# Delta rule of a transformer block: the triangular inverse on 32x32 blocks instead of 64x64

## The chip, the cores and the metric

One NeuronCore of one Trainium2 chip runs the whole program. The metric is device time in microseconds (us), the median of several runs. The kernel is written by hand, engine by engine, with semaphores: TensorE (PE in the profile), VectorE (DVE), ScalarE (ACT), GpSimd (POOL) and SyncE (SP), which issues the weight loads.

## The reference, cut to what matters

The reference is a stack of transformer layers on 256 context and 256 latent tokens, d_model 1024, with four feed-forward blocks. One of its mixers has an RWKV-7 half: 8 heads of 64 channels, each run once forward and once backward over the tokens.

```python
def step(S, inp):
    r, w, k, v, kk, a = inp
    S = (S * w[:, :, None, :]
         - jnp.einsum('bhvk,bhk->bhv', S, kk)[..., None] * (kk * a)[:, :, None, :]
         + v[..., None] * k[:, :, None, :])
    return S, jnp.einsum('bhvk,bhk->bhv', S, r)
```

The kernel does not step through tokens. It cuts them into 8 chunks of 64. Inside a chunk the rule becomes a linear system with a unit triangular 64x64 matrix I + A, where A holds products of decayed keys ("alpha", "beta"). The inverse of that matrix is applied to two right sides, and 8 chunk states are then chained.

## The kernel before, in words

The part that the change touches is called wkv in the code. Its work is 4 groups g (groups 0 and 1 forward, 2 and 3 backward). A group is two units u = 0, 1, and a unit is a pair of heads (128 partitions hold two heads, or two token halves). For each unit all 8 chunks of both heads are treated at once: 16 triangular matrices of 64x64, laid out as 8 cells of 64 columns on two partition halves (128x512). TensorE runs each group in three stages in a fixed order written by hand:

- **Start** (`wkv_start_tensor`). `within(n)` makes the 16 products beta x alpha and the 16 products alpha x beta (`products`, L2112, matmuls of 64x64x64). `turn` transposes the three factors (L2123), ScalarE copies them (L2281). Then come products with kappa and rho (`mixes`, L2112) and `key_values` (L2135). VectorE masks the results (L2423 to L2438), and starts the inverse: TI and its transpose TTI, both 128x512.
- **Levels** (`wkv_levels_tensor`). Five levels with block sizes 2, 4, 8, 16 and 32 double the block that is already inverted. Level li of unit u: GpSimd masks the strict triangle AT to the off-block of this level (MB, L2323, 128x512); TensorE multiplies MB by TI (`square`, L2177); ScalarE copies the product to XS (L2288); TensorE multiplies TTI by XS and XS by TTI; VectorE subtracts the two products from TI and TTI (L2445, L2446). The last level makes the second product alone. A `square` is 16 matmuls of 64x64x64, on the two diagonal 64x64 quadrants of the array. So a group has 28 squares.
- **Ends** (`wkv_ends_tensor`). TTI is applied to both right sides (L2208, L2213), ScalarE copies the solutions with a minus sign (L2302, L2303), and TensorE makes the outputs of the unit (L2224 to L2233) and the factors of the states (L2242 to L2251) from products on all four quadrants. VectorE adds the outputs (L2454, L2456) and the identity to the state factors (L2462). `within` of the next group waits for that.

After groups 1 and 3, `wkv_scan_tensor` (L2086, L2089) chains the 8 chunk states.

Beside that, the factors of the next group are prepared: two small products for decays and rates (`wkv_low_ranks`, L2100, L2101, in levels 0 and 2), sigmoids on ScalarE (`wkv_rates_scalar`), sums over the tokens on VectorE (`wkv_decay_sums`, L2413, L2415), exponentials on ScalarE (`wkv_decays_scalar`, L2272 to L2274), and products on GpSimd (`wkv_keys`, `wkv_factors`, `wkv_rho`, L2357 to L2378). The rates of the two units share one set of tiles, so unit 1 follows unit 0.

Every f32 matmul of this part stands in the trace as two MATMUL and two LDWEIGHTS records. "Records" below are MATMUL records. None of this part is in a hardware loop: every matmul is an instruction of its own in the program.

Of the kernel before, what the change touches and what calls it, by code (L numbers as in the profile page):

```python
# [27 lines left out]
P = 128  # L28
# [4 lines left out]
TT = T // P  # L33
# [10 lines left out]
CHUNK = 64  # L44
NCH = T // CHUNK
# [10 lines left out]
          ("sel_f", 64), ("mu", 7 * P), ("ml", 7 * P), ("cu", 6 * HD), ("cl", 6 * HD), ("su", HD), ("sl", HD), ("iu", HD),  # L56
          ("il", HD),
# [195 lines left out]
def build(nc, xin, ctx2, condrows, stream_k, stream_f, vecs, consts, tables, small, nabias, out):  # L253
# [4 lines left out]
    with ExitStack() as ctx:  # L258
# [1632 lines left out]
        NG1, NG2 = TI, MB  # L1891
# [9 lines left out]
        def rate_tiles(n):  # L1901

            return (SIG1, CUM1, AA1) if n == 1 else (SIG0, CUM0, AA0)
# [117 lines left out]
        LAST = len(BLOCK_LEVELS) - 1  # L2021

# [21 lines left out]

        def bank_pair(b, q):

            return banks[:, b:b + 2, q * 4 * HD:(q + 1) * 4 * HD].rearrange("p h (t c) -> p h t c", c=HD)

        def on_cells(mask):

            return mask.unsqueeze(1).unsqueeze(1).to_broadcast([P, 2, TT, HD])
# [52 lines left out]
        def wkv_start_tensor(pe, g):  # L2104
# [9 lines left out]

            def within(n):
# [34 lines left out]
            pe.wait_ge(factors_by_token, 3 * n0 + 1)  # L2150
            turn(n1, 1, 4)
            pe.wait_ge(factors_by_token, 3 * n0 + 2)
# [9 lines left out]
            pe.wait_ge(factors_by_token, 3 * n1 + 1)  # L2162
            mixes(n1, 6)
            pe.wait_ge(mixes_masked, n0 + 1)
            pe.wait_ge(factors_by_token, 3 * n1 + 2)
            key_values(n0, 4)
            pe.wait_ge(mixes_masked, n1 + 1)
            pe.wait_ge(factors_by_token, 3 * n1 + 3)
            key_values(n1, 5)

        def wkv_levels_tensor(pe, g):

            def square(bank, x, y):
                for i in range(2 * TT):
                    for half in HALF:
                        o = slice(i * HD, (i + 1) * HD)
                        mm = pe.matmul(pb[bank][half, o], x[half, o], y[half, o], start=True, stop=True)  # L2177
                return mm

            for li in range(len(BLOCK_LEVELS)):  # L2180
                for u in range(2):
                    q = NLEV * g + 2 * li + u
                    pe.wait_ge(level_masked, q + 1)
                    if li:
                        pe.wait_ge(t_updated, q - 1)
                    else:
                        pe.wait_ge(t_started, 2 * g + u + 1)
                    square(u, MB[u], TI[u]).then_inc(x_ready, 1)
                if g < 3 and li in (0, 2):
                    wkv_low_ranks(pe, 2 * g + 2 + li // 2)  # L2190
                for u in range(2):
                    pe.wait_ge(x_copied, NLEV * g + 2 * li + u + 1)
                    if li == 0:
                        pe.wait_ge(rho_masked, g + 1)
                        pe.wait_ge(kv_copied, 2 * g + u + 1)
                    if li < LAST:
                        square(2 + u, TTI[u], XS[u])
                    square(4 + u, XS[u], TTI[u]).then_inc(z_ready, 1)

        def wkv_ends_tensor(pe, g):  # L2200
            for u in range(2):
                pe.wait_ge(t_updated, NLEV * (g + 1) - 1 + u)
                if u and g < 3:
                    pe.wait_ge(rates_ready, 2 * g + 4)
                for tt in range(TT):
                    for hb in range(2):
                        for half in HALF:
                            pe.matmul(pb[2 + 4 * u][half, cell(hb, tt)], TTI[u][half, cell(hb, tt)],  # L2208
                                      TOKA[u][half, chunk(tt, hb)], start=True, stop=True)
                for tt in range(TT):  # L2210
                    for hb in range(2):
                        for half in HALF:
                            mm = pe.matmul(pb[3 + 4 * u][half, cell(hb, tt)], TTI[u][half, cell(hb, tt)],  # L2213
# [41 lines left out]
        def wkv_rates_scalar(act, n):  # L2255
# [5 lines left out]
            if n >= 2:  # L2261
                act.wait_ge(factors_ready, n)
# [13 lines left out]
        def wkv_scalar(act):  # L2276
            for g in range(4):
                for u in range(2):
                    for i, (by_token, bank) in enumerate(zip((TOKA, TOKB, TOKK), ((4, 5, 6), (7, 4, 5))[u])):
                        act.wait_ge(factors_turned, 3 * (2 * g + u) + i + 1)  # L2280
# [4 lines left out]
                for li in range(len(BLOCK_LEVELS)):  # L2285
                    for u in range(2):
                        act.wait_ge(x_ready, NLEV * g + 2 * li + u + 1)
                        act.activation(XS[u], pb[u][:, :], ACT.Copy).then_inc(x_copied, 1)  # L2288
                    if g == 3 and li < 4:
                        act.wait_ge(mixed_copied, pairs_before(1))  # L2290
                        act.activation(out_hi(0, li), H[:, li, :], ACT.Copy).then_inc(mixer_hi, 1)
                    if g < 3 and li == 0:
                        wkv_rates_scalar(act, 2 * g + 2)
                    if g < 3 and li == 2:
                        wkv_decays_scalar(act, 2 * g + 2)
                    if g < 3 and li == 4:
                        wkv_rates_scalar(act, 2 * g + 3)
# [6 lines left out]
                if g < 3:  # L2304
                    wkv_decays_scalar(act, 2 * g + 3)
# [8 lines left out]
        def wkv_gpsimd(pool):  # L2314

            def masks(g, li):
                level = C("cu" if g < 2 else "cl", LEVELS.index(BLOCK_LEVELS[li]) * HD, HD)
                for u in range(2):
                    if li:
                        pool.wait_ge(x_ready, NLEV * g + 2 * li + u - 1)  # L2320
                    else:
                        pool.wait_ge(triangles_ready, 2 * g + u + 1)
                    pool.tensor_tensor(cells(MB[u]), cells(AT[u]), on_cells(level), ALU.mult).then_inc(level_masked, 1)  # L2323
# [7 lines left out]
            for g in range(4):  # L2331
                n0 = 2 * g + 2
                masks(g, 0)
                masks(g, 1)
                if g < 3:
                    wkv_keys(pool, n0)
                masks(g, 2)
                masks(g, 3)
                if g < 3:
                    wkv_factors(pool, n0)  # L2340
                    if g != 1:
# [1277 lines left out]
```

## Time and profile before

| | |
|---|---|
| time, median of 3 runs | 2647.64 us (2647.13 to 2650.81) |
| span of the profiled execution | 2655.0 us |
| the four wkv groups, without the scan between groups 1 and 2 | 242.42 us |
| one group: start, levels, ends (group 0) | 12.26, 33.40, 15.54 us |
| TensorE busy | 2489.5 us, 94% |
| VectorE, ScalarE, GpSimd busy | 1696.8, 1059.9, 418.4 us |

For the profiled execution no time is given beside its span of 2655.0 us; the span is 7.4 us above the median of the other runs. TensorE's matmuls are pipelined and the ends of their records are modelled: a share of 94% says that it is seldom idle, not that it works at its peak. Where it is idle and the trace shows no one that it waits for, the profile writes "issue".

### The profile page before, as it was taken

To read this page: it belongs to the slowest core of one execution; us is meant where nothing else is said; L and a number is where in the kernel's file an instruction comes from. 1 tells how busy PE (TensorE), PEld (TensorE's weight loads), DVE (VectorE), ACT (ScalarE), POOL (GpSimd) and SP (SyncE) were. 2 spreads that over 40 slices of the span, in tenths; PEclk is the share of its full clock that TensorE was granted. 3 is DMA by queue.
4 is the path that set the end of the run, shared out by engine and by line. 5 is a ranking of instruction groups with operands and counts; after the bars stand their busy time and mean duration, and the time that the engine had idled before them with its cause. 6 is when DMAs were issued, how large, how long until landed. Compare 5 with 4: busy or idle time off the path is not lost.

```text
span 2655.0 us, 49488 instructions
## 1 busy us (share of the span) xinstructions
PE 2489.5 (94%) x19578; PEld 2041.4 (77%) x19578; DVE 1696.8 (64%) x2787; ACT 1059.9 (40%) x1750; POOL 418.4 (16%) x372
## 2 busy tenths in 40 slices
PE   6999999988888999999999999889999998899977
PEld 4888888757777778888788888669997875577857
DVE  2877787565554687778887754665555334565664
ACT  4222224454333542222522223455455343455344
POOL 2000001024445300000100001001013600121042
PEclk9999999989999999999999999999999999899999
DMA  7766662200000166666466652315563321023401
GB/s 264 226 194 193 195 204 94 81 5 4 4 4 12 56 195 192 193 194 201 157 205 193 194 149 89 98 51 159 181 180 104 96 91 40 1 64 123 126 14 48
DMA packets 88434, 323.55 MB, mean 122 GB/s; under 512 B 9712, under 2 KB 10864, under 8 KB 87504
## 3 DMA queue, kind: packets, MB, share of 16 engines
q1 hardware_dynamic: 86864, 310.68, 38.0%
q0 software_dynamic: 1408, 10.59, 1.1%
q8 instruction: 117, 1.92, 0.3%
q14 instruction: 45, 0.37, 0.0%
HBM read 320.18 MB, written 1.05 MB: 121 GB/s over the span
## 4 chain that ended last, share of the span: by engine, by line
PE 80%; DVE 9%; ACT 5%; issue 4%; DVEq 1%; DMA 1%; POOL 0%; POOLq 0%; ACTq 0%; SPq 0%
PE bank L502 21%; PE bank L504 21%; PE bank L503 21%; PE bank L2177 4%; PE bank L1389 1%; PE bank L1380 1%; DVE row_statistics L1434 1%; DVE weights_hi_lo L408 1%; PE bank L1405 1%; ACT work L1495 1%; ACT weights_hi_lo L403 1%; DMA weight_ring<-stream_k 1%; PE bank L1809 1%; ACT work L1504 1%; PE bank L2800 1%
## 5 line engine op out<-in xcount | busy, mean ns | idle before, releaser
L403 ACT ACTIVATE weights_hi_lo<-weight_ring 128x1024 fp32r<-128x1024 f32 (+1 forms) x381 | 396.7, 1042 | 1085.7 <-PE bank L504 1060.7
L408 DVE TENSOR_TENSOR weights_hi_lo<-weight_ring,weights_hi_lo 128x1024 fp32r<-128x1024 f32 (+1 forms) x374 | 454.6, 1216 | 481.4 <-ACT weights_hi_lo L403 479.7
L502 PE MATMUL bank<-input_hi,weights_hi_lo 128*128 128x512 f32 (+1 forms) x2032 | 743.8, 366 | 18.9 <-DVE input_lo L813 12.3
L503 PE MATMUL bank<-input_lo,weights_hi_lo 128*128 128x512 f32 (+1 forms) x2032 | 740.3, 364 | 0.0
L504 PE MATMUL bank<-input_hi,weights_hi_lo 128*128 128x512 f32 (+1 forms) x2032 | 740.1, 364 | 0.0
L502 PEld LDWEIGHTS bank<-input_hi,weights_hi_lo 128*128 128x128 f32 x2032 | 386.6, 190 | 85.7 <-issue 22.9
L503 PEld LDWEIGHTS bank<-input_lo,weights_hi_lo 128*128 128x128 f32 x2032 | 386.7, 190 | 60.2 <-issue 0.7
L504 PEld LDWEIGHTS bank<-input_hi,weights_hi_lo 128*128 128x128 f32 x2032 | 386.5, 190 | 59.9
L502 PE MATMUL bank<-hidden_hi_lo,weights_hi_lo 128*128 128x512 f32 (+1 forms) x952 | 343.5, 361 | 5.0 <-DVE hidden_hi_lo L1109 2.1
L504 PE MATMUL bank<-hidden_hi_lo,weights_hi_lo 128*128 128x512 f32 (+1 forms) x952 | 340.2, 357 | 0.0
L503 PE MATMUL bank<-hidden_hi_lo,weights_hi_lo 128*128 128x512 f32 (+1 forms) x952 | 340.2, 357 | 0.0
L754 POOL TENSOR_TENSOR work<-work 128x512 f32<-128x512 f32 (+1 forms) x48 | 70.6, 1470 | 1233.1 <-ACT work L642 1232.1
L552 DVE CUSTOM_DVE_ANT_0 work<-weight_ring,extra_tiles 128x1024 f32<-128x1024 f32 x176 | 224.6, 1276 | 35.8 <-issue 13.3
L553 DVE CUSTOM_DVE_ANT_0 weight_ring<-weight_ring,extra_tiles 128x1024 f32<-128x1024 f32 x176 | 214.9, 1221 | 0.0
L502 PEld LDWEIGHTS bank<-hidden_hi_lo,weights_hi_lo 128*128 128x128 f32 x952 | 181.2, 190 | 35.0 <-DVE hidden_hi_lo L1109 4.0
L503 PEld LDWEIGHTS bank<-hidden_hi_lo,weights_hi_lo 128*128 128x128 f32 x952 | 181.3, 190 | 26.0 <-issue 0.7
L504 PEld LDWEIGHTS bank<-hidden_hi_lo,weights_hi_lo 128*128 128x128 f32 x952 | 181.1, 190 | 25.6
L1279 DVE TENSOR_TENSOR work<-work,bank 128x512 f32<-128x512 f32 (+1 forms) x88 | 54.7, 622 | 54.4 <-PE bank L504 45.6
L1434 DVE TENSOR_REDUCE row_statistics<-bank 128x2 f32<-128x1024 f32 (+2 forms) x56 | 55.7, 995 | 38.8 <-PE bank L1380 36.8
L1495 ACT ACTIVATE work<-bank,row_statistics 128x512 f32<-128x512 f32 (+1 forms) x80 | 47.4, 598 | 68.3 <-DVE row_statistics L1434 47.2
L1389 PEld LDWEIGHTS bank<-constants,work 128*128 128x128 f32 x256 | 32.9, 160 | 51.0 <-issue 43.2
L2323 POOL TENSOR_TENSOR work<-work,constants 128x512 f32<-128x512 f32 x40 | 51.9, 1304 | 96.6 <-PE bank L2177 52.0
(515 smaller groups left out, 3110.9 us busy)
## 6 DMA issues: line engine op xcount, KB each, us to landing
weight_ring<-stream_k SPq DMA_DIRECT2D x498, 512.0 KB, 3.7
weight_ring<-stream_f SPq DMA_DIRECT2D x64, 448.0 KB, 3.4
weight_ring<-stream_f SPq DMA_DIRECT2D x32, 512.0 KB, 3.7
extra_tiles<-condrows POOLq DMA_DIRECT2D x3, 1024.0 KB, 9.3
constants<-consts POOLq DMA_DIRECT2D x1, 2112.5 KB, 9.0
residual_stream<-xin SPq DMA_DIRECT2D x1, 2048.0 KB, 12.1
work<-nabias POOLq DMA_DIRECT2D x1, 2048.0 KB, 8.9
residual_stream<-ctx POOLq DMA_DIRECT2D x1, 1024.0 KB, 6.2
```

What stands on the lines that cost most here:

```text
L403: act.activation(split_place(place)[:, 0, 0:words], w[:, 0:words], ACT.Copy).then_inc(hi_ready, 1)
L408: eng.tensor_tensor(split_place(place)[:, 1, 0:words], ring[:, n % RING, 0:words], split_place(place)[:, 0, 0:words].bitcast(F32), ALU.sub ...
L502: pe.matmul(out, weights[:, 0, w], x_hi, start=first, stop=False)
L503: pe.matmul(out, weights[:, 0, w], x_lo, start=False, stop=False)
L504: return pe.matmul(out, weights[:, 1, w], x_hi, start=False, stop=last)
L552: dve.tensor_tensor_reduce(PRODUCTS, w, COND[:, 0, :], 1.0, 0.0, ALU.mult, ALU.add, MOD_SUMS[:, j, 0:1])
L553: dve.tensor_tensor_reduce(w, w, COND[:, 1, :], 1.0, 0.0, ALU.mult, ALU.add, MOD_SUMS[:, j, 1:2]) .then_inc(mod_read, 1)
L754: pool.tensor_tensor(total, total, squares_of(place, kt)[:, a:b], ALU.add)
L1389: mm = pe.transpose(pb[4 + b][:, tok(i)], attention_probs(which, u)[:, b, tok(i)], C("ident"))
L1434: ins = dve.tensor_reduce(st[:, 0, :], sc[:, :, 0:nk], AX.X, ALU.max, negate=True)
L1495: ins = act.activation(attention_probs(which, it)[:, b, 0:nk], pb[2 * (it % 2) + b][:, 0:nk], ACT.Exp, bias=st[:, 0, b:b + 1], accum_out=s ...
L2177: mm = pe.matmul(pb[bank][half, o], x[half, o], y[half, o], start=True, stop=True)
```

## The change

- The recursion runs on 32x32 diagonal blocks alone. `within` becomes `near_products`: the two diagonal 32x32 blocks of each 64x64 matrix, in both orders, and a third set, the blocks beside the diagonal. These are matmuls with 64 rows, 32 weight columns and 32 moving columns.
- Levels 0 to 3 (block sizes 2 to 16) work on tiles of 128x256 (HALF_T = 256), four 32-row quarters with 8 blocks each. `square` becomes 32 matmuls of 32x32x32 on the four diagonal 32x32 tiles of the array.
- The last level computes only the block beside the diagonal: `across` and `across_turned` (16 matmuls each), and `near_blocks`, which moves the diagonal blocks to their place in a 128x512 bank by 32 matmuls with the identity and 16 with zeros. ScalarE copies that bank to INVERSE (in AT's tile), VectorE copies the off-blocks beside it.
- The copies XS go from ScalarE to VectorE, at 128x256; the updates of TI and TTI have a semaphore count each.
- GpSimd's masks (now 128x256) run up to two levels ahead, in two halves of MB, and all four levels of masks stand ahead of the rest of its work.
- Both units' rates are made together during the levels (in tiles of their own), then both `wkv_keys` on GpSimd. Both `wkv_decay_sums` stand behind the levels on VectorE, both `wkv_decays_scalar` behind the copies of the solutions on ScalarE, and `wkv_factors`, `wkv_rho` of both units follow on GpSimd.

```diff
+            def near_products(b, o, x, y, beside):
+                for tt in range(TT):
+                    for k in range(4):
+                        for hb in range(2):
+                            rows, i, j = HALF[hb], tt * P + k * SUB, tt * P + (k ^ beside) * SUB
+                            mm = pe.matmul(pb[b + hb][QUARTER[k], o + tt * SUB:o + (tt + 1) * SUB], x[rows, i:i + SUB],
+                                           y[rows, j:j + SUB], start=True, stop=True)
...
-                products(2 * (n % 2), 0, be, al)
-                products(2 * (n % 2), 1, al, be).then_inc(within_ready, 1)
+                near_products(2 * (n % 2), 0, be, al, 0)
+                near_products(2 * (n % 2), P, al, be, 0)
+                near_products(2 * (n % 2), 2 * P, be, al, 1).then_inc(within_ready, 1)
...
-            def square(bank, x, y):
+            def square(bank, x, x0, y):
                 for i in range(2 * TT):
-                    for half in HALF:
-                        o = slice(i * HD, (i + 1) * HD)
-                        mm = pe.matmul(pb[bank][half, o], x[half, o], y[half, o], start=True, stop=True)
+                    for rows in QUARTER:
+                        mm = pe.matmul(pb[bank][rows, near(i)], x[rows, x0 + i * SUB:x0 + (i + 1) * SUB], y[rows, near(i)],
+                                       start=True, stop=True)
+            def across(u):
+                for i in range(2 * TT):
+                    for k in first_rows(d):
+                        mm = pe.matmul(pb[u][QUARTER[k ^ 1], near(i)], AT[u][QUARTER[k], HALF_T + i * SUB:HALF_T + (i + 1) * SUB],
+                                       TI[u][QUARTER[k], near(i)], start=True, stop=True)
+            def near_blocks(u):
+                for i in range(2 * TT):
+                    for k, rows in enumerate(QUARTER):
+                        o = i * HD + k % 2 * SUB
+                        pe.matmul(pb[4 + u][rows, o:o + SUB], C("id32")[rows, :], TTI[u][rows, near(i)], start=True, stop=True)
+                for i in range(2 * TT):
+                    for k in first_rows(1 - d):
+                        o = i * HD + (1 - k % 2) * SUB
+                        mm = pe.matmul(pb[4 + u][QUARTER[k], o:o + SUB], C("id32")[QUARTER[k], :], C("zero32")[QUARTER[k], :],
+                                       start=True, stop=True)
...
 def wkv_scalar(act):
     for g in range(4):
...
-                for li in range(len(BLOCK_LEVELS)):
-                    for u in range(2):
-                        act.wait_ge(x_ready, NLEV * g + 2 * li + u + 1)
-                        act.activation(XS[u], pb[u][:, :], ACT.Copy).then_inc(x_copied, 1)
...
+                if g < 3:
+                    act.wait_ge(x_ready, NLEV * g + 2)
+                    wkv_rates_scalar(act, 2 * g + 2)
+                    wkv_rates_scalar(act, 2 * g + 3)
...
+                for u in range(2):
+                    act.wait_ge(z_ready, near_read(g, u))
+                    act.activation(INVERSE[u], pb[4 + u][:, :], ACT.Copy).then_inc(factors_by_token, 1)
...
+                    wkv_decays_scalar(act, 2 * g + 2)
                     wkv_decays_scalar(act, 2 * g + 3)
...
 def wkv_group_vector(dve, g):
...
-                    dve.wait_ge(z_ready, NLEV * g + 2 * li + u + 1)
                     if li < LAST:
-                        dve.tensor_tensor(TI[u], TI[u], pb[2 + u][:, :], ALU.subtract)
-                    dve.tensor_tensor(TTI[u], TTI[u], pb[4 + u][:, :], ALU.subtract).then_inc(t_updated, 1)
+                        dve.tensor_copy(XS[u][:, 0:HALF_T], pb[u][:, 0:HALF_T]).then_inc(x_copied, 1)
...
+                        dve.tensor_tensor(TI[u][:, 0:HALF_T], TI[u][:, 0:HALF_T], pb[2 + u][:, 0:HALF_T], ALU.subtract)\
+                           .then_inc(t_updated, 1)
```

## Rows read from the trace of the kernel before

**Rows 1.** The page, part 1: busy time, share of the span, records of TensorE.
```profile
PE 2489.5 (94%) x19578; PEld 2041.4 (77%) x19578; DVE 1696.8 (64%) x2787; ACT 1059.9 (40%) x1750; POOL 418.4 (16%) x372
```
**Rows 2.** Windows: busy (records) of PE, PEld, DVE, ACT, POOL. Group 0, group 3's levels.
```profile
605.88:618.14 12.26, 10.70 (x407) 9.67 (x409) 9.86 (x16) 3.75 (x7) 2.56 (x2) 1.00 0.02 4
618.14:651.54 33.40, 31.23 (x912) 28.18 (x908) 14.55 (x19) 13.12 (x19) 18.92 (x16) 1.00 0.02 4
651.54:667.08 15.54, 10.24 (x519) 9.72 (x514) 7.31 (x9) 7.70 (x13) 9.64 (x8) 1.00 0.02 4
...
814.60:844.50 29.90, 27.27 (x902) 26.75 (x900) 10.97 (x17) 9.59 (x16) 16.82 (x12) 1.00 0.02 4
```
**Rows 3.** The chain that ended last: us from the start, us, what. Levels of group 0.
```profile
642.33 4.89 PE bank L2177 x160
647.25 0.69 DVE spare_tiles L2445
...
648.68 3.02 PE bank L2177 x96
```
**Rows 4.** The same chain, in the ends of group 0.
```profile
657.70 0.47 PE bank L2224 x32
...
659.32 1.64 issue
660.96 0.46 PE bank L2242 x17
...
663.05 1.64 issue
```
**Rows 5.** Windows between these two stalls, TensorE alone.
```profile
657.23:659.35 2.12, 2.09 (x128) 1.00 0.04 8
660.95:663.08 2.13, 2.09 (x128) 1.00 0.03 8
```
**Rows 6.** DMA queue of the instructions: packets, MB; group 0, then one stall's period.
```profile
q8 instruction: 14, 0.23, 1.7%
q8 instruction: 1, 0.02, 2.2%
```
**Rows 7.** The chain, stalls in the ends of group 1.
```profile
720.95 1.36 issue
724.40 1.36 issue
```
**Rows 8.** Windows of whole groups, the first and the last of four, and their sum.
```profile
605.88:667.08 61.20, 52.17 (x1825) 47.58 (x1825) 31.72 (x44) 24.57 (x38) 31.11 (x26) 1.00 0.02 4
801.90:860.60 58.70, 53.18 (x1856) 48.73 (x1856) 25.97 (x42) 19.40 (x33) 33.28 (x23) 1.00 0.05 13
sum 242.42, PE 210.69 PEld 192.76 DVE 121.42 ACT 93.22 POOL 126.44; mean PE 52.67 PEld 48.19 DVE 30.36 ACT 23.30 POOL 31.61
```
**Rows 9.** Timeline, TensorE: 16 records in tiles of 128x32.
```profile
410.62 0.64 PE L488 MATMUL bank<-weight_ring,modulation 128*32 128x128 f32 x16
```
**Rows 10.** Source line L1467: VectorE's copy of 128x128 out of PSUM, ns min/median/max.
```profile
L1467 DVE COPY mixer_io<-bank x40: 277/285/292, 558.8 to 2571.0; 128x128 f32<-128x128 f32 x40
```
**Rows 11.** Windows with TensorE's granted clock (PEclk, 1.00 is full).
```profile
728.70:740.80 12.10, 7.57 (x208) 6.61 (x208) 8.39 (x20) 0.00 (x0) 0.00 (x0) 1.00 0.01 3
544.40:551.20 6.80, 4.97 (x16) 2.40 (x16) 3.54 (x8) 1.93 (x8) 0.00 (x0) 0.50 0.00 0
667.00:669.00 2.00, 1.92 (x65) 1.83 (x66) 0.00 (x0) 0.00 (x0) 0.00 (x0) 0.56 0.00 0
```
**Rows 12.** Timeline of group 0's ends: start, us, engine, what, idle before.
```profile
653.08 1.22 DVE L2413 TENSOR_TENSOR_SCAN work<-spare_tiles,work 128x512 f32<-128x512 f32 x1 [0.65 <-ACT work L2264]
654.37 1.54 DVE L2415 TENSOR_TENSOR work<-work 128x512 f32<-128x512 f32 x1
...
659.68 1.26 POOL L2368 TENSOR_TENSOR spare_tiles<-spare_tiles,projections 128x512 f32<-128x512 f32 x1 [1.72 <-ACT spare_tiles L2274]
665.69 1.29 DVE L2462 TENSOR_TENSOR projections<-bank,spare_tiles 128x512 f32<-128x512 f32 x2 [5.23 <-PE bank L2251]
```

More of the change, by code:

```diff
@@ L2021, in build @@
         LAST = len(BLOCK_LEVELS) - 1
+        NIN = 2 * LAST
+        NUPD = 4 * LAST + 4
+        NTOK = 8
+        QUARTER = [slice(SUB * k, SUB * k + SUB) for k in range(4)]
+        HALF_T = 2 * TT * SUB
         CORNERS = [(0, 0), (1, 1), (0, 1), (1, 0)]
@@ L2043, in by_half, with near, near_cells, near_bank_pair @@
             return ap.rearrange("p (t h c) -> p h t c", h=2, c=HD)
+        def near(i):
+            return slice(i * SUB, (i + 1) * SUB)
+        def near_cells(ap):
+            return ap[:, 0:HALF_T].rearrange("p (h t c) -> p h t c", h=2, c=SUB)
+        def near_bank_pair(b, o):
+            return banks[:, b:b + 2, o:o + TT * SUB].rearrange("p h (t c) -> p h t c", c=SUB)
+        def plain_update(g, li, u):
+            return NUPD * g + 4 * li + 2 * u + 1
+        def turned_update(g, li, u):
+            return NUPD * g + 4 * li + 2 * u + 2
+        def near_read(g, u):
+            return NUPD * g + 4 * LAST + u + 1
+        def across_read(g, u):
+            return NUPD * g + 4 * LAST + 2 + u + 1
+        def across_added(g, u):
+            return (NUPD - 2) * g + 4 * LAST + u + 1
+        def first_rows(d):
+            return (0, 2) if d == 0 else (1, 3)
         def bank_pair(b, q):
@@ L2178, in square, with across_turned @@
+            def across_turned(u):
+                for i in range(2 * TT):
+                    for k in first_rows(d):
+                        mm = pe.matmul(pb[u][QUARTER[k], near(i)], XS[u][QUARTER[k ^ 1], near(i)],
+                                       TTI[u][QUARTER[k ^ 1], near(i)], start=True, stop=True)
                 return mm
@@ L2195, in wkv_levels_tensor @@
                         pe.wait_ge(kv_copied, 2 * g + u + 1)
+                    elif li < LAST:
+                        pe.wait_ge(t_updated, turned_update(g, li - 1, u) - 2 * g)
                     if li < LAST:
-                        square(2 + u, TTI[u], XS[u])
-                    square(4 + u, XS[u], TTI[u]).then_inc(z_ready, 1)
+                        square(2 + u, TTI[u], 0, XS[u]).then_inc(z_ready, 1)
+                        square(4 + u, XS[u], 0, TTI[u]).then_inc(z_ready, 1)
+                    else:
+                        across_turned(u).then_inc(z_ready, 1)
         def wkv_ends_tensor(pe, g):
             for u in range(2):
-                pe.wait_ge(t_updated, NLEV * (g + 1) - 1 + u)
+                pe.wait_ge(t_updated, across_added(g, u))
+                pe.wait_ge(factors_by_token, NTOK * g + 6 + u + 1)
                 if u and g < 3:
```

139 lines of the change are left out of this document (82 added, 57 removed).

## Prediction, made before the changed kernel was run

> **What bounds the kernel now.** I read the page first: TensorE is busy 94% of the span [rows 1], so a stage is worth what it costs TensorE. Then the windows by stage. The four wkv groups take 242.42 us together [rows 8]; group 0 is 12.26 us of start, 33.40 of levels, 15.54 of ends [rows 2]. The reader should see that GpSimd, VectorE and ScalarE are busy for only 19, 15 and 13 of the 33.4 us of levels. The chain of waits there gives the pattern: TensorE runs 160 records in 4.89 us, VectorE's update of 0.69 and one more of some 0.6 follow, and the next stretch starts 6.35 us after the last (648.68 - 642.33) [rows 3]. A level has six squares of 32 records, 192 records; 4.89/160 = 30.6 ns a record with the run-out of the last one, about 29 without, 0.93 us a square; 6 of them leave some 0.7 us of a level in which TensorE waits or runs out. So the levels wait on TensorE, and the masks and copies are hidden. The two low-rank products cost 3.5 us: the levels of group 3, which has none, take 29.90 [rows 2].
>
> The decisive view is the chain in the ends. There the matmuls use four quadrants: 32 records in 0.47 us, 14.7 ns each. And twice TensorE stops for 1.64 us in the middle of a run of matmuls that waits for nobody, put down as "issue" [rows 4]. It starts again at 660.96 and at 664.69 (663.05 + 1.64), 3.73 us apart. Between two stops stand exactly 128 records [rows 5], and each has a weight load: 256 instructions. The queue that loads instructions brings one packet of 0.02 MB in such a period, and 14 in the group [rows 6], whose 1825 matmuls and 1825 weight loads [rows 8] make 14.3 times 256. I read this as follows: TensorE's program arrives in blocks of 256 instructions, and a new block takes about 3.6 us whatever the engine does meanwhile. The same stops in group 1: 720.95 + 1.36 and 724.40 + 1.36 are 3.45 us apart [rows 7]. The levels now use up a block in 128 x 29 ns = 3.7 us, just what the supply gives: they are at this limit already, without showing it.
>
> **The change, part by part.**
>
> *Levels on 32x32.* A square goes from 16 matmuls to 32, so from 32 records to 64. Each is shorter. No row shows a 32x32 tile; the nearest are these. A record with 64 moving columns holds its quadrant for 4 x 14.7 = 59 ns [rows 4]. 16 records in 32-column tiles with 128 moving columns take 0.64 us in all [rows 9], where one behind the other, at twice 59 ns, they would take 1.9: four tiles of this width run side by side. A record with 32 moving columns should hold its tile for half of 59 ns and a little more; I take 33, an estimate. Four quarters side by side make 8.2 ns a record, 0.52 us a square. Bounds: 14.7 ns (0.94 us a square, no gain) if a small record costs as much as one of 64 columns on four quadrants, and 33 ns (2.1 us) if the quarters do not overlap. I take 8.2 because [rows 9] shows such tiles overlap. The dependencies would allow a level of 6 x 0.52 plus 0.2 for the copy, 3.3 us instead of 6.35.
>
> *Last level.* across 32 records, near_blocks 96, across_turned 32, for two units 320, where 4 squares had 128. Levels in all: 24 squares x 64 + 320 = 1856 records instead of 28 x 32 = 896: +960. *within*: 3 x 64 instead of 2 x 32 for each unit: +256. Nothing else changes in number. So +1216 records per group on 1825, +4864 in all.
>
> *Copies on VectorE.* A 128x128 copy is 0.285 us [rows 10], an update of 128x512 0.69 [rows 3]; at 128x256 between, some 0.40. Six per level, 2.4 us: hidden behind even the short level of 3.3 us, and further behind a level that waits for instructions. In the longest case, 0.69 each, they are 4.1 us. Masks: GpSimd's share falls and runs ahead; now they are hidden too (18.9 of 33.4 us with all its other work [rows 2]). No gain or loss on TensorE's path.
>
> *Rates together, decays behind the levels.* After the levels VectorE makes two sums (1.22 + 1.54 each [rows 12]), 5.5 us, where it made one; ScalarE's exponentials of both units come after the copies of the solutions, the last of which ends some 5 us in (solves of 128 records at 29 ns, 3.7 us, then two copies), so at about 6.5 to 10 us into the ends; then GpSimd has two times factors (three products of 1.26 [rows 12]) and rho, until some 18 us. `within` of unit 0 needs its factors at 15.5 us, and they are there at 12; unit 1's are needed a `within` and three transposes later, 1.5 blocks or 5 us, at 21. So it is covered, by 3 us; without that cover (no instruction limit) it would be needed at about 19 and the margin would be 1 to 2 us. Queued behind the late sums on VectorE are the output adds; TensorE's wait on them ends only with L2462 at 665.69 [rows 12], 8 us later. Cost nothing; at worst 2 us a group.
>
> *The sum.* All four groups now have 1824 x 3 + 1856 = 7328 records; after it 12192, or 24384 instructions, 95.25 blocks. At 3.6 us a block (between the 3.45 of group 1 [rows 7] and the 3.73 of group 0 [rows 4]) that is 342.9 us. Minus 5 for the blocks that are at hand when group 0 and, after the scan, group 2 begin (two times 3.6 less 1.0 to run them); plus 2 for the wait on L2462 at the end of each group where it does not fall into a block's wait (0.5 each). 340 against 242.4 [rows 8]: +98. A block of the levels takes TensorE 1 us of work and at most 1.5 us of waits for copies, under 3.6, so that none of the dependencies adds.
>
> *Clock.* TensorE is at work for 1 us in 3.6 there. After the idle time before L2462 the clock was granted at 0.56 (1.2 GHz for most of the window), in sparse attention work at 0.50, but in the scan, where TensorE gets 208 short records in 12.1 us, it stayed at 1.00 [rows 11]. In the levels half a clock is hidden (2 us a block). It costs in the two-quadrant solves of the ends: a block of 128 records takes 7.4 us instead of 3.7. I count this in a third of cases: 4 x 3.7 / 3 = +5.
>
> So +103 us: the profiled execution 2655 + 103 = 2758; the median of the runs, 2647.6, lies 7.4 us below the profile's span, so 2751.
>
> *A, the supply of instructions is no limit* (the other side). The stops in the ends would come from something else, or blocks would arrive ahead. For it: in the levels there is hardly any stop now. Against: 128 records between stops, twice, and one instruction packet. Then levels 0 to 3 take 4 x 3.3, the two low-rank products 3.5, the last level 4.6 (320 records of 8 to 16 ns and a copy at each end, about its 4 squares of now): 21.3 instead of 33.4; within costs +1.3 (2 x (192 x 8.2 - 64 x 14.7) ns); -10.8 a group, -43: 2604 us. It decides once a block arrives in less than 61 us / 23.8 blocks = 2.5 us. The page "Runtime: NRT & Kernel Launch" of the Trainium skill, section "Instruction fetch mechanics", says the same: blocks of 256 instructions, fetched while the current one runs, the crossing "mostly hidden". The trace agrees on the block, and differs on the hiding [rows 4, 5]; the measurement decides.
>
> *B, a small record costs as much as a large one, and A.* 14.7 ns a record, levels 1856 x 14.7 = 27.3, with 3.5 and 2.5 of waits 33, as now; within +3.8 a group, +15: 2663 us. For it: no row below 14.7 ns holds for long.
>
> *C, the clock falls in every group*: solves +3.7, and the two low-rank blocks 3.5 more together with some 0.5 for key_values: 4 x 7.7 = +31 on the +98: 2776 us.
>
> *D, the quarters do not overlap*: 2240 records of levels and within at 33 ns are 73.9 us a group, by blocks 63.0: +11 a group, +44: 2789 us.
>
> **Numbers.** Forecast (blocks of 3.45 to 3.73 us, clock mostly full) 0.64; C 0.2; D 0.04; A 0.07; B 0.05. At 3.45 us a block the sum is 328.6 - 3 = 325.6, +83: 2731; at 3.73 355.3 - 3 = 352, +110, with C's 31 +141: 2789. The bounds of the unknown: packets that come somewhat faster when they are the only limit (3.3 us: 314 - 3, +69: 2716). Range 2712 to 2796. A measurement here tells 0.2%, 5 us, from no change. Slower: 0.64 + 0.2 + 0.04 + 0.05 = 0.93; faster 0.06, same 0.01 (A, with the late factors taking back all of its gain).
>
> **What would show it.** In the profile after: about 24400 / 256 = 95 instruction packets over the groups, a group of 83 to 90 us, levels of some 52 us and a start of some 18; stops put down as "issue" of 1.5 to 2.6 us every 128 records through the levels; squares of 0.5 us between them; VectorE, ScalarE and GpSimd waiting for TensorE. The prediction is wrong if levels run 192 times 2 records in clearly under 10 us, if packets come closer than 3.3 us, or if copies on VectorE end TensorE's waits.

## The result, and the profile after

The changed kernel takes 2774.12 us (median, 2772.39 to 2777.97), the kernel before 2648.62 (2647.13 to 2650.81) beside it: 1.0477 times as long (95% interval 1.046 to 1.0493). The prediction, 2751 us and a range of 2712 to 2796, was right in sign and range and 23 us short. One execution of the kernel with split columns below (2790.17 us) and one of the kernel before (3577.27 us) ran in a slower state, and every figure here leaves them out.

The page of the changed kernel: span and busy time of each engine (part 1), part 2's strip of 40 slices for TensorE and its granted clock, the instruction queue (part 3), and the shares of the chain (part 4).

```profile
span 2771.7 us, 59255 instructions
PE 2513.5 (91%) x24442; PEld 2057.9 (74%) x24442; DVE 1688.4 (61%) x2843; ACT 1036.6 (37%) x1712; POOL 387.5 (14%) x364
PE   6999999976676699999999999987999999889977
PEclk9999999996676599999999999999999999999999
q8 instruction: 155, 2.54, 0.4%
PE 78%; DVE 7%; issue 7%; ACT 4%; DMA 1%; DVEq 1%; POOL 0%; POOLq 0%; ACTq 0%; SPq 0%
```

Compare with [rows 1]: TensorE has 4864 more records and is busy for only 24 us more, while the span is 117 us longer. The digits show where: in the six slices that hold most of wkv TensorE is busy for 60 to 79%, and the granted clock falls with it. From 590 to 990 us the chain of waits holds 54 stops of more than 1.3 us put down as "issue", 99 us together, where that of before holds 6, 9 us together; these 90 us more are most of the 117. The packets of the instruction queue are the best check on what a packet is. The page of before counts 117. 38 more came, and 4864 records with as many weight loads, 9728 instructions, are 38.0 times 256.

Windows by stage: the four starts, the four levels, the four ends (first and last of each, and the sum of the four), and the whole group 0.

```profile
602.30:620.10 17.80, 13.83 (x664) 12.62 (x664) 8.84 (x18) 3.97 (x7) 3.02 (x4) 0.90 0.02 5
...
sum 78.52, PE 59.05 PEld 54.15 DVE 35.52 ACT 16.32 POOL 22.67; mean PE 14.76 PEld 13.54 DVE 8.88 ACT 4.08 POOL 5.67
620.10:676.10 56.00, 34.92 (x1869) 29.15 (x1864) 11.83 (x28) 5.61 (x8) 9.46 (x10) 0.58 0.02 4
...
909.28:960.73 51.45, 29.26 (x1860) 27.29 (x1856) 11.86 (x29) 4.82 (x8) 18.70 (x14) 0.56 0.02 5
sum 217.71, PE 132.44 PEld 113.35 DVE 47.37 ACT 21.65 POOL 47.06; mean PE 33.11 PEld 28.34 DVE 11.84 ACT 5.41 POOL 11.77
676.10:691.35 15.25, 11.79 (x513) 11.41 (x513) 8.44 (x12) 7.78 (x13) 5.25 (x6) 0.88 0.02 5
...
960.73:980.50 19.77, 16.53 (x520) 13.63 (x520) 5.01 (x9) 5.07 (x9) 4.86 (x3) 0.85 0.10 31
sum 68.77, PE 52.32 PEld 48.10 DVE 31.32 ACT 28.42 POOL 23.63; mean PE 13.08 PEld 12.03 DVE 7.83 ACT 7.10 POOL 5.91
602.30:691.35 89.05, 60.54 (x3041) 53.18 (x3041) 29.11 (x58) 17.36 (x28) 17.73 (x20) 0.69 0.02 4
```

Against [rows 2] a start grew from 12.26 to 17.80 us, levels from 33.40 to 56.00 (group 3: 29.90 to 51.45). Group 0's ends hardly changed (15.54 to 15.25), but in groups 1 to 3 they grew from 14.9 to 16.1 us before to 17 to 20. The four groups take 365.0 us (the three sums) instead of the 242.42 of [rows 8]: +122.6. The levels hold 87 us of it.

The chain of waits in the levels of group 0 (start us, us, what), where [rows 3] had stretches of 96 to 160 records and VectorE's updates between them:

```profile
628.33 2.09 issue
630.42 1.39 PE bank L2232 x106
631.80 2.68 issue
634.49 1.93 PE bank L2232 x127
636.41 1.79 issue
638.20 1.93 PE bank L2232 x95
640.13 2.34 issue
642.47 1.93 PE bank L2232 x127
644.40 2.06 issue
```

Windows of TensorE alone between these stops, the counterpart of [rows 5]:

```profile
634.49:638.20 3.71, 1.92 (x127) 0.50 0.02 4
638.20:642.47 4.27, 1.93 (x128) 0.50 0.02 4
642.47:646.46 3.99, 1.93 (x127) 0.50 0.02 4
```

This is the stop of [rows 4] again and again: 127 or 128 records, a stop that nobody ends, the next block 3.7 to 4.3 us after the last. L2232 is the 32x32 square. Who is waiting for whom around it, from the timeline (in brackets the idle time before, and who ended it):

```profile
634.49 0.79 PE L2232 MATMUL bank<-spare_tiles,work 32*32 32x32 f32 x41 [2.68 <-issue]
635.31 0.42 DVE L2536 COPY spare_tiles<-bank 128x256 f32<-128x256 f32 x1 [3.28 <-PE bank L2232]
635.36 0.73 POOL L2416 TENSOR_TENSOR work<-work,constants 128x256 f32<-128x256 f32 x1 [2.98 <-PE bank L2232]
636.17 0.42 DVE L2542 TENSOR_TENSOR work<-work,bank 128x256 f32<-128x256 f32 x1 [0.43 <-PE bank L2232]
```

VectorE had been idle for 3.28 us and GpSimd for 2.98, both waiting for TensorE; the copy XS on VectorE takes 0.42.

### The profile page after: what moved, and what is told of

Its sections match the earlier page's. It is cut to its first block, busy times and chain, and to the rows that moved or that the text cites. A ratio compares the mean times of both kernels' runs of the same rounds, so it can differ in the third digit from the quotient of the medians.

```text
span 2771.7 us, 59255 instructions
## 1 busy us (share of the span) xinstructions
PE 2513.5 (91%) x24442; PEld 2057.9 (74%) x24442; DVE 1688.4 (61%) x2843; ACT 1036.6 (37%) x1712; POOL 387.5 (14%) x364
## 3 DMA queue, kind: packets, MB, share of 16 engines
HBM read 320.01 MB, written 1.05 MB: 116 GB/s over the span
## 4 chain that ended last, share of the span: by engine, by line
PE 78%; DVE 7%; issue 7%; ACT 4%; DMA 1%; DVEq 1%; POOL 0%; POOLq 0%; ACTq 0%; SPq 0%
PE bank L503 20%; PE bank L504 20%; PE bank L505 20%; PE bank L2232 3%; PE bank L1390 1%; DVE weights_hi_lo L409 1%; DVE row_statistics L1435 1%; DMA weight_ring<-stream_k 1%; PE bank L1381 1%; ACT work L1496 1%; ACT weights_hi_lo L404 1%; PE bank L1406 1%; ACT work L1505 1%; PE bank L1810 1%; PE bank L2177 1%
## 5 line engine op out<-in xcount | busy, mean ns | idle before, releaser
L2232 PE MATMUL bank<-work 32*32 32x32 f32 x3072 | 48.3, 225 | 24.5 <-issue 24.5
L2232 PEld LDWEIGHTS bank<-work 32*32 32x32 f32 x3072 | 43.1, 138 | 33.6 <-issue 33.2
```

The lines of the kernel that those rows point to most:

```text
L2232: mm = pe.matmul(pb[bank][rows, near(i)], x[rows, x0 + i * SUB:x0 + (i + 1) * SUB], y[rows, near(i)], start=True, stop=True)
```

## The experiments

Two theories are weighed. One is the supply of instructions, as predicted. The other is that the records themselves hold TensorE, by what each costs. In the expectations F is the first theory and R the second. Each median is given with its range; every ratio is against the kernel before, measured beside it.

### Twice the instructions, the arithmetic unchanged

Before's `square`, with each 64-column matmul as two of 32 columns:

```diff
-                    for half in HALF:
-                        o = slice(i * HD, (i + 1) * HD)
-                        mm = pe.matmul(pb[bank][half, o], x[half, o], y[half, o], start=True, stop=True)
+                    for c in range(2):
+                        for half in HALF:
+                            o, m = slice(i * HD, (i + 1) * HD), slice(i * HD + 32 * c, i * HD + 32 * c + 32)
+                            mm = pe.matmul(pb[bank][half, m], x[half, o], y[half, m], start=True, stop=True)
```

> Kernel before, each square's matmul cut into two that move 32 of its 64 columns: same result, same columns, twice the instructions in the levels (+896 records, 7 blocks of 256 instructions a group). Theory F (the program arrives in blocks of 256 instructions, one per 3.5 to 3.8 us): a group has 2720 records, 21.25 blocks, 77 to 81 us instead of 61: +64 to +80 us, 2712 to 2729. Rival R (no limit on the supply; TensorE's columns and dependencies set the time): 32 columns hold a quadrant for 33 ns instead of half of 59, a square takes 1.06 us instead of 0.93: +15 us, 2663.

2743.05 us (2738.62 to 2746.11), 1.0347 (1.032 to 1.0374). The chain in the levels of group 0, and the window of its longest stretch:

```profile
616.52 1.05 PE bank L2100 x2
617.57 0.86 PE bank L2101 x2
618.43 22.52 PE bank L2178 x768
```
```profile
618.43:640.95 22.52, 22.52 (x770) 22.48 (x769) 7.47 (x10) 3.09 (x6) 7.41 (x6) 1.00 0.02 4
```

The time is far above R's 2663 us and 14 us above the top of F's range, and F's mechanism is not there: group 0's levels have no stop. 768 records in 22.52 us are 29.3 ns each, without one stop, at a granted clock of 1.00. That is the pace per record of [rows 3], where a record moves twice the columns. A record with 64 weight columns holds its quadrant for 59 ns whether it moves 32 or 64 columns. A block of 128 such records takes 3.75 us, within the supply's 3.3 to 4.3, so this run can't tell the two theories apart. It does show what R had wrong: halving the columns did not bring a record's 59 ns to 33.

### Half the columns, as many instructions

The square moves 32 of each 64 columns, and ScalarE and VectorE read each computed half twice. ScalarE's copy is scaled by 0, so in two squares of three one operand is all zeros:

```diff
-                        o = slice(i * HD, (i + 1) * HD)
-                        mm = pe.matmul(pb[bank][half, o], x[half, o], y[half, o], start=True, stop=True)
+                        o, m = slice(i * HD, (i + 1) * HD), slice(i * HD, i * HD + 32)
+                        mm = pe.matmul(pb[bank][half, m], x[half, o], y[half, m], start=True, stop=True)
...
-                        act.activation(XS[u], pb[u][:, :], ACT.Copy).then_inc(x_copied, 1)
+                        act.activation(halved(XS[u]), first_half(pb[u][:, :]), ACT.Copy, scale=0.0).then_inc(x_copied, 1)
```

> Kernel before, each square moves only 32 of its 64 columns; ScalarE's copy of the product is scaled by 0 and copies and updates read the written half twice, so the levels' result is left out and the inverse stays what it was at its start. Same instructions, half the columns. F: a level has 192 records, 1.5 blocks, so it can't fall below 5.4 us (6.35 before): -12 to -18 us, 2631 to 2637. R: squares of 0.53 us, the level then follows copies and updates, 4.7 us: -30 us or more, 2618 or less.

2713.58 us (2703.14 to 2719.24), 1.0246 (1.0226 to 1.0266): slower with half of the columns, which no theory had. A window of the second half of group 0's levels:

```profile
637.50:661.50 24.00, 24.00 (x451) 24.00 (x452) 5.83 (x9) 4.94 (x7) 7.71 (x8) 0.50 0.01 2
```

TensorE never stops in it, and its clock was granted at 0.50 (1.2 GHz). At 24.00/451 = 53 ns a record, two quadrants side by side, each is held for 106 ns, nearly twice the 59 of full clock. The levels of group 0 took 47.9 us. As a test of supply against records it is inconclusive; it shows what half a clock costs where nothing else limits.

Why the clock fell is open, and the narrower records alone don't explain it: the run before this one has records of the same shape, as tightly packed, at 1.00 for 22.52 us. Two things differ. Here one operand is zero in two squares of three; and before the clock fell, at about 624 us, TensorE had stood for 1.4 us (from 621.26) while VectorE made its two updates. Neither was tried alone; the written-out kernel below has such zeros too, and its clock from 620 to 676 us was 0.58, as without them. With these records it then stayed at 0.50 for the rest of the levels without a stop, and rose at about 665 us, in the solves, which move 64 columns.

### The new square with wider columns

The changed kernel, each 32x32 matmul moving 64 columns instead of 32:

```diff
+                        if i < 2 * TT - 1:
+                            m = slice(i * SUB, (i + 2) * SUB)
+                        else:
+                            m = slice((i - 1) * SUB, (i + 1) * SUB)
-                        mm = pe.matmul(pb[bank][rows, near(i)], x[rows, x0 + i * SUB:x0 + (i + 1) * SUB], y[rows, near(i)],
+                        mm = pe.matmul(pb[bank][rows, m], x[rows, x0 + i * SUB:x0 + (i + 1) * SUB], y[rows, m],
```

> Kernel after, each of its squares in levels 0 to 3 moves 64 columns instead of 32 (overlapping outputs, so the inverse is wrong): same instructions, twice the columns. F: a block of the levels needs about 2 us of TensorE at full clock, still under the 3.6 us in which the next arrives: no change, 2768 to 2782; if the additional activity keeps the clock up, up to 15 us faster. R: 1536 records a group cost 6.5 ns more at full and 13 at half clock, 10 to 20 us a group: +40 to +80 us, 2814 to 2854.

2772.31 us (2768.7 to 2773.76), 1.0458 (1.0439 to 1.0476), so no change against the changed kernel's 2774.12. The window of group 0's levels, and a stop and the block behind it from the chain:

```profile
619.75:675.75 56.00, 39.11 (x1868) 34.11 (x1865) 11.84 (x29) 5.61 (x8) 9.45 (x10) 0.82 0.02 4
```
```profile
642.00 1.98 PE bank L2236 x127
643.98 2.00 issue
```

56.00 us, as in the changed kernel, though the records do twice the columns and are busy for 39 us instead of 35. The clock was granted at 0.82 instead of 0.58, and that bought nothing. Neither the width of a record nor the clock sets the levels' time. R had 2814 us or more; here it is out.

### Fewer instructions: 48 matmuls of each unit moved to other engines

The changed kernel without `near_blocks` on TensorE: ScalarE copies the diagonal blocks to their place, GpSimd sets the zeros.

```diff
-                        near_blocks(u).then_inc(z_ready, 1)
...
-                    act.activation(INVERSE[u], pb[4 + u][:, :], ACT.Copy).then_inc(factors_by_token, 1)
+                    for k, rows in enumerate(QUARTER):
+                        ins = act.activation(block_of(u, k, k % 2), tiles(TTI[u][rows, 0:HALF_T], SUB), ACT.Copy)
...
+                    for k in first_rows(1 - g // 2):
+                        ins = pool.memset(block_of(u, k, 1 - k % 2), 0.0)
```

> Kernel after, without the 48 matmuls per unit that only move the diagonal blocks and zeros into place in the last level: ScalarE copies TTI's four quarters to their place instead, GpSimd writes the zeros. Same result. 192 records fewer a group, 1.5 blocks. F (supply of instructions): -1.5 x 3.7 us a group less a small wait for ScalarE's eight short copies, -14 to -22 us, 2752 to 2760. R (TensorE's own time): 192 records of 10 to 15 ns, and the new copies stand on the path: 0 to -10 us, 2764 to 2774.

2745.7 us (2742.52 to 2749.7), 1.037 (1.0349 to 1.0392): 28 us faster than the changed kernel, with 768 records less. Its page has `q8 instruction: 149`, 6 packets fewer than 155, and 2 x 768 / 256 is 6. At 3.8 us a packet (365.0 us over 95 blocks) that is 23 us. The time lies 18 us below R's range, but also 6 us below F's; where the other 5 us went is not shown.

### The same matmuls, in a loop and written out

Two kernels with the same matmuls, the same output and the same VectorE work, made from the changed one. Each runs the first four blocks of a square twice and one matmul more; the other four blocks are left out. In the first the repetition is a hardware loop, in the second it is written out:

```diff
-                with pe.Fori(0, 2):
+                for _ in range(2):
                     for i in range(TT):
                         for rows in QUARTER:
                             one(i, rows)
```

> Kernel after, each square of levels 0 to 3 runs the matmuls of its first four blocks in a hardware loop of two turns, 64 instructions in the body (the other four blocks are left out, VectorE reads the first half twice and scales the copy by 0). TensorE executes as many matmuls as before (one more per square), but the program holds about 56 instructions less per square, 1344 a group, 5.2 blocks. F, if a turn of the loop stays within what is loaded: -19 us a group, -76 us, about 2698; if each turn back waits for a block anew, +86 us a group. R: the stops go with executed instructions: 2774 to 2785.

> Control of e8: the same matmuls in the same order (the first four blocks of each square twice, one more matmul at the end, VectorE reading the first half twice and scaling the copy by 0), but written out without the hardware loop, so the program holds all of them. F: as the kernel after plus 24 x 2 records a group, 2774 to 2783, with the stops every 128 records back; e8 stays 40 us or more below. If e8's gain came from its data or from what it leaves out, e9 is as fast as e8, 2729.

Loop: 2729.3 us (2726.19 to 2735.2), 1.0305 (1.0285 to 1.0326). Written out: 2783.51 (2780.19 to 2788.05), 1.05 (1.0476 to 1.0523). 54 us lie between them. The chain in the levels of the loop, the window of these levels, and the instruction queue of its page:

```profile
629.17 1.04 PE bank L2239 x63
630.22 0.05 issue
630.27 1.11 PE bank L2239 x62
631.37 0.12 issue
631.49 1.03 PE bank L2239 x63
```
```profile
617.50:662.00 44.50, 40.02 (x1947) 32.16 (x1939) 13.79 (x31) 5.33 (x8) 9.46 (x10) 0.76 0.01 3
```
```profile
q8 instruction: 134, 2.20, 0.3%
```

A stop in the same chain, written out, and the instruction queue of its page:

```profile
631.54 2.25 issue
```
```profile
q8 instruction: 157, 2.57, 0.4%
```

In the loop the levels' stops of 2 us are gone (the longest left in group 0's levels is 1.04) and "issue" falls from 34.5% of the levels' chain to 11.3%. Its page counts 134 packets, 23 fewer than 157: 96 squares run 32 matmul records each from instructions already there, with their weight loads 6144 instructions, 24 times 256. Only how the instructions come differs between these two kernels. This is the run that shows the cause. From 590 to 990 us the chain holds 55 stops of more than 1.3 us written out, 98 us together, and 15 in the loop, 27 us together.

F's number for the loop was about 2698 us, and 2729 came. F took the supply to be the limit still, at 3.8 us for each of the 23 packets, 88 us. But in these levels TensorE works for 40.02 of 44.50 us, and a square in the loop takes 1.03 us for 63 records at full clock (16 ns each) where straight code has 0.75 us for 64: its own pace limits there now. Why a record costs more in the loop was not tried. Even so, the loop's kernel is 3% slower than before: no version here gains by small tiles.

### The moves alone, and one count alone

First, before with the moves of the change: XS copied on VectorE, both rates together, decays behind the levels, and TI's update counted alone. Second, before with that count only, so that the next level's first square doesn't wait for TTI's update:

```diff
-                        pe.wait_ge(t_updated, q - 1)
+                        pe.wait_ge(t_updated, NUPD * g + 4 * (li - 1) + 2 * u + 1)
...
-                        dve.tensor_tensor(TI[u], TI[u], pb[2 + u][:, :], ALU.subtract)
+                        dve.tensor_tensor(TI[u], TI[u], pb[2 + u][:, :], ALU.subtract).then_inc(t_updated, 1)
```

> Kernel before with the parts of the change that add no instruction on TensorE: copies XS on VectorE (still 128x512), both units' rates together, decay sums and exponentials behind the levels, a count of its own for the update of TI. F: TensorE's records are those of before, so the time stays near before: the separate count saves up to 0.5 us a level, the copy behind VectorE's last update gives back 0.2 or more: 2638 to 2652. Rival M (the moves are what costs): some 5 us or more a group later factors: over 2665.

> Kernel before with one thing of the change: the update of TI is counted by itself, so that the next level's first product waits for it alone and not for TTI's update behind it. F and R alike: TensorE's idle time of about 0.5 us before unit 1 of levels 1 to 4 goes, 16 times: -8 us, 2641; under F a level has 1.5 blocks and stays above 5.4 us, so stops may come back for some of it: -4 to -8, 2641 to 2645.

The moves with the count: 2645.28 us (2641.85 to 2648.27), 0.9985 (0.9972 to 0.9998). The count alone: 2639.09 (2635.81 to 2642.33), 0.9964 (0.9951 to 0.9977). A window of group 0's levels with the count:

```profile
614.68:645.69 31.01, 30.96 (x910) 28.04 (x906) 14.55 (x19) 13.13 (x19) 19.29 (x16) 1.00 0.02 4
```

33.40 us [rows 2] became 31.01: TensorE's waits and run-outs (33.40 - 31.23 = 2.2 us in all) are gone, and it is busy for 30.96. Rival M (over 2665) is out. The moves' own cost is the difference of the two, 6 us, near what this measurement can tell (the two intervals just overlap).

### Versions without more instructions

Three kernels built on the count alone. First, both right sides in one matmul of 128 moving columns, 64 records a group less:

```diff
-                            pe.matmul(pb[2 + 4 * u][half, cell(hb, tt)], TTI[u][half, cell(hb, tt)],
-                                      TOKA[u][half, chunk(tt, hb)], start=True, stop=True)
...
+                            mm = pe.matmul(banks[half, 2 + 4 * u + hb, tt * P:(tt + 1) * P], TTI[u][half, cell(hb, tt)],
+                                           both_sides(u, half, hb, tt), start=True, stop=True)
```

> As e6, and the two right sides are solved by one matmul of 128 moving columns instead of two of 64: same result, same columns, 64 records fewer a group (half a block). F: the stops in the ends shrink by half a block's 3.7 us a group: -7 us against e6, about 2634. R: same columns on the same quadrants, no gain against e6: 2641.

2638.9 us (2634.36 to 2641.84), 0.9964 (0.9951 to 0.9976): nothing beyond the count that can be measured. F's further 7 us did not come, though its page has 115 packets instead of 117: half a block fewer a group did not shorten the stops.

Then, on the count alone, the last level computes only the block beside the diagonal, with as many matmuls as before, on the 64-wide tiles and without a fifth mask:

```diff
-                    square(u, MB[u], TI[u]).then_inc(x_ready, 1)
+                    (square(u, MB[u], TI[u]) if li < LAST else across(u)).then_inc(x_ready, 1)
...
+                    for k in first_rows(g // 2):
+                        mm = pe.matmul(pb[u][QUARTER[k ^ 1], side(i, k)], AT[u][QUARTER[k], side(i, k ^ 1)],
+                                       TI[u][QUARTER[k], side(i, k)], start=True, stop=True)
```

> As e6 (before, TI's update counted by itself), and the last level computes only the 32x32 block beside the diagonal, on the 64-wide storage: as many matmuls as before, with 32 rows, 32 weight and 32 moving columns; GpSimd's last mask is not needed, VectorE updates 32 partitions at a time. Same result. R: four squares of 0.93 us become four of 0.53, less waits that come free: -1.2 us a group, -5 against e6, 2634. F: the last level is one block of instructions as before; what it gains is given back at the stops of the ends: 0 to -3 against e6, 2636 to 2640.

> e10 and the merged solve of e7. F: half a block fewer in the ends pays now for the time won in the last level: -3 to -6 us against e6, 2633 to 2637. R: as e10, 2634.

Alone 2637.48 us (2634.91 to 2639.49), 0.995 (0.9933 to 0.9967); with the merged solve 2635.21 (2630.96 to 2640.99), 0.9946 (0.9928 to 0.9965). The levels of group 0 in the last:

```profile
613.42:643.53 30.11, 29.70 (x910) 26.52 (x907) 14.71 (x21) 12.89 (x19) 16.83 (x14) 1.00 0.02 4
```

30.11 instead of 31.01; in groups 1 and 2 the levels became 0.7 and 1.0 us shorter. As a step beyond the count it is not settled, since the intervals overlap. As a whole this last kernel is the fastest here, 0.5% ahead of before, and it keeps the 64x64 squares.

## Why the prediction was right, and where it was short

**The supply of instructions.** Right, and shown. Stops every 127 or 128 records; twice the columns and a higher granted clock (0.82 instead of 0.58) change nothing; 6 packets less give 28 us; and the same matmuls in a loop are 54 us faster. Rival A (2604 us) is out. Of the signs named beforehand, the packets (23 in group 0), the levels of 51 to 56 us and the engines that wait for TensorE came; the groups were longer (89 to 93 us, not 83 to 90) and so were the squares (0.75 us, not 0.5). That the levels of before ran at this limit without showing it is not shown: in the kernel with the count alone and in the one with split columns a block takes 3.75 us or so because records with 64 weight columns take 29 ns each, and the supply keeps up. The two limits lie side by side there, and my reading of [rows 3] by itself could not have told them apart. The page "Runtime: NRT & Kernel Launch" of the Trainium skill, section "Instruction fetch mechanics", calls the crossing of a block mostly hidden. The loop against the written-out kernel shows the opposite for TensorE at this pace, 54 us for 23 packets.

**Its size, the term that was short.** The step "at 3.6 us a block" gave 340 us for 95.25 blocks with leads and tails. The four groups took 365.0 for 95 blocks (3040 records each), 3.84 us a block; the distances seen run from 3.7 to 4.3 in group 0's middle and down to

```profile
655.54:659.02 3.48, 1.92 (x127) 0.50 0.02 5
659.02:662.35 3.33, 1.92 (x127) 0.50 0.02 5
```

further on. Two stops of before in each of two groups were a thin base for a single figure. By stage, against four times the 18 and 52 us that the prediction named and the rest of its 340: starts 78.5 instead of 72, levels 217.7 instead of 208, ends 68.8 instead of 60. Why the distance between blocks varies was not tried.

**The clock.** It fell in every group, as in rival C: 0.56 to 0.64 in the levels. In the wider-column run it fell less, and the levels took 56.00 again, so inside blocks that wait it costs nothing, as predicted. What it costs stands behind the levels, in the chain:

```profile
676.14 2.03 PE bank L2301 x32
678.17 1.71 PE bank L2306 x32
679.88 0.96 PE bank L2301 x32
680.84 0.88 PE bank L2306 x30
```

The solves of the first unit took 2.03 + 1.71 us, those of the second 0.96 + 0.88: +1.9 us, half of the 3.7 that I had put on a group at half clock. In the starts, which I had not priced, each of the eight stretches of transposes (`turn`, 12 records) took 1.46 us where the clock was full and up to 2.75 where it was 0.50; six of the eight were longer than 1.46, by 6.7 us together (in before one was, 2.30). How much of this the supply would have taken anyway is not shown. The second pair of low-rank products of groups 0 to 2 took 3.71 us instead of 1.91, with the same reservation. So the clock's part lies between some 8 us (the solves alone) and 20, where the sum had 5.

What came is therefore rival C's mechanism (given 0.2) and not that of the main forecast, "clock mostly full" (given 0.64). That C's 2776 us lies 2 us from the measured 2774 is luck all the same: its 31 us for the clock was too high (it also counted low-rank products in group 3, which has none), and its 3.6 us a block too low.

**From 2751 to 2774.** The groups: 365.0 - 345 (340 and the 5) = 20 us. Between groups 1 and 2, where the scan is: before 12.30, after 13.20 us, +1. The rest of the program took 6.8 us less in this profiled execution (3.6 before wkv begins, at 602.30 instead of 605.88, and 3.2 after its end). Together 14, in the span: 2771.7 against 2758. The other 10 is the step from span to median: I took 7.4 us off, but the median of after lies 2.4 us above its profile's span. The two belong together. Where both are on record, an execution's time is some 2 us above its span (2773.64 for 2771.7). So the profile of before came from an execution of some 2657 us, 8 to 9 above the median, and it was slow outside the groups: in the trace with the count alone wkv begins at 602.36, in that of split columns at 600.34. The medians differ by 125.5 us, the groups by 122.6.

**The squares.** I took 8.2 ns a record, 0.52 us a square. The first square of group 0's levels and its neighbour ran 64 records in

```profile
620.15 0.75 PE L2232 MATMUL bank<-work 32*32 32x32 f32 x64
```

11.7 ns each with the run-out of the last; at half clock 1.93 us for 127 are 15.2 ns. So the four quarters do overlap (D is out: 33 ns). The 0.52 us was too low, and it cost nothing, since the levels wait for instructions. B's time (2663) hung on A and is out with it.

**The moves.** "Cost nothing; at worst 2 us a group", the prediction said. In before they cost some 6 us for four groups, under that bound; in the changed kernel VectorE and GpSimd wait 3 us for TensorE, and they are hidden. The copy on VectorE took 0.42 us (0.40 predicted). The one part of the change that pays is the separate count, which I had not priced at all: its place is VectorE's two updates of 0.69 and 0.61 us in a row, in front of the next level's first square. It is worth 9.4 us, 0.36%.

## What to carry to other kernels

Count instructions before you cut matmuls smaller: a straight run of them was fed here at one block of 256 per 3.3 to 4.3 us, 3.84 on average. My estimate from this: below some 30 ns a record with its weight load (3.84 us / 128) little is gained. A change that makes each square shorter and doubles its instructions lost here. Look in the trace for stops of "issue" every 128 records where the matmuls are at their shortest, and hold the packets of the instruction queue against the count. If small tiles are wanted, try them in a hardware loop, which gave back 54 us here, and measure against the kernel without them. And first count updates separately, which takes no instruction on TensorE.

## What the runs showed of the hardware that was not expected

- A record with 64 weight columns and 64 or 32 moving columns held its quadrant for 59 ns at full clock (768 in 22.52 us on two quadrants), and with 32 moving columns for 106 ns at half (451 in 24.00 us). My reading is that the weight load sets this pace; no run changed the weight columns alone. The page "TensorE: Matmul & The Clock Gate" of the Trainium skill, section "LDWEIGHTS (loading the stationary operand)", has a weight load go by its columns alone; its formula gives 53 ns for 64. The 59 ns of full clock are near that, the 106 of half clock are not.
- An unbroken run of matmuls stayed at a granted clock of 0.50 for 24 us, while records of the same shape in another kernel kept 1.00 for 22.52 us. What decides between the two was not found; the kernel at half clock was 2.5% slower than before (ratio 1.0246, 1.0226 to 1.0266).
- In the changed kernel the clock was granted at 0.50 in blocks in which TensorE worked for 1.93 us of every 3.7 to 4.3. With records of twice the columns it was 0.82 over the same levels, at the same total time.
- Turning back in a hardware loop of 64 instructions brought no stop: the two turns of a square stand as one piece in the chain, with 0.05 to 0.12 us of "issue" between squares. But a record took 16 ns at full clock instead of 12.
